# A decoder layer's middle: state space stage, sample attention and mixing as one program with interleaved engine orders

## The chip, the cores and the metric

The kernel runs on one core of one Trainium2 chip. The metric is the device time of one execution in microseconds (us), the median of the runs; less is better. A core has five engines that run on their own and meet only at semaphores: TensorE (PE, with its weight loads as PEld), VectorE (DVE), ScalarE (ACT), GpSimd (POOL) and SyncE (SP), which here issues most DMAs. All data are fp32.

## What is computed

One inference step of a hybrid decoder layer for a prompt of 1024 positions and a sample group of 8 sequences with 4 new positions each (32 rows). What matters here is the first sub-layer. One projection gives q, k, v and u; 12 heads of 64 in three groups attend with dilation 1, 4 and 16; u drives a diagonal state space model; both outputs are normalised, concatenated and go through w_out.

```python
def parallel_mixer(xn, pos, past_kv, s0_re, s0_im, p):
    z = xn @ p['w_in']                       # q | k | v | u
    ...
    for g, (win, dil) in enumerate(ATTN_GROUPS):      # (128,1), (512,4), (2048,16)
        if past_kv is None:
            o, lse = dilated_attn_prompt(qg, kg, vg, win, dil)
        else:                                # keys and values of the cache, then the new ones
            o, lse = dilated_attn_sample(qg, k_all, v_all, win, dil, buf.shape[1])
        outs.append(o); lses.append(lse)
    alpha = jax.nn.softmax(jnp.stack(lses, axis=2), axis=2)
    attn = jnp.stack(outs, axis=2) * alpha[..., None]
    y, h_re, h_im = s5_scan(u, s0_re, s0_im, p)       # h' = a h + b u ; y = Re(C h) + D u
    zs = jax.nn.gelu(y)
    ssm_out = zs * jax.nn.sigmoid(zs @ p['w_glu'] + p['b_glu'])
    mixed = concat([rmsnorm(attn), rmsnorm(ssm_out)])
    return mixed @ p['w_out'], ...
```

The outputs also include the last states of the model for the prompt and for each sample. After this come cross attention and a ConvFFN.

## The kernel before, in words

`build` calls one function per stage. Each opens a `Block`, in which every engine has its own instruction list, in the order in which the Python code emits it; no engine looks ahead in its own list, waits are semaphore thresholds (`wait_ge`), and all engines meet at the end of a block. The stages are `block_project` (L100: projection and prompt attention), `block_ssm` (L629), `block_sample` (L1153), `block_mix` (L1419), then `block_dense` for w_out, the memory projection and w_xq, cross attention, w_xo, and the FFN. This case is about the three in the middle. SBUF tensors of each are placed by nested scopes, and the eight PSUM banks are reused by all.

`block_ssm`. SP issues 10 loads for lambda, dt and B (L718 to L726), then C, the start states, D, the GLU weights and the gains (L730 to L737); TensorE and GpSimd wait for all 13 of the latter with one semaphore (`ld`). VectorE and ScalarE turn lambda and dt into a = exp(lambda dt) (L880 to L896; the sine wants another activation table). VectorE makes powers of a, B' and its chunk form BAR/BAI (L872 to L945, `bb`) and C times powers, CAR/CAI (to L957). GpSimd multiplies U by D (L766) and makes the table ER/EI of a^(8k) for the 128 chunks by doubling (L776 to L781, six instructions per complex product, two products per doubling). TensorE transposes C and the states (L1031, L1033), U (L1038), the sample's U (L1043) and BAR/BAI (L1050), makes the Toeplitz blocks (L1061), which SP spreads into TZ with 8 DMAs (L747), and the chunk sums (L1072, L1080). VectorE rotates the sums by the table (L966), scans them (L981, L982) and rotates back into HR/HI. TensorE then transposes the last states (L1088), computes the prompt's outputs (L1097 to L1100) and the sample's (L1108, L1110). GELU, the GLU product (L1121) with its sigmoid, and the norm (L1023) follow, each in a loop over 9 tiles of rows (8 of the prompt, 1 of the sample).

`block_sample`. 48 loads of cached keys (24) and then values (24) go through a ring of 12 slots, `ringS`; a slot is loaded again when TensorE has used what it held. The groups have 1, 4 and 2 blocks of 128 keys per sequence, 56 in all. For each, TensorE transposes two halves into one of four banks (L1363), ScalarE or VectorE in turn copies them to one of 8 places in `kTcS` (L1266, L1322), and TensorE multiplies three blocks later (L1372). The scores are transposed once, masked and put through a softmax over 128 partitions (L1330 to L1341), transposed back, and the values are weighed (L1409). Meanwhile GpSimd squares the attention outputs of the prompt (L1247), VectorE reduces them (L1315), and GpSimd sends the statistics through DRAM into row order (L1149).

`block_mix`. VectorE works out the mixing weights and norms (L1495 to L1519), then scales the 24 tiles of prompt attention (L1524), GpSimd multiplies by the gain (L1464), TensorE transposes each of 36 tiles (9 of the state space model, 3 of the sample, 24 of attention; L1542), ScalarE writes the high part XH (L1476) and VectorE the rest XL (L1492), through four banks. SP loads the first block of w_out.

Of the kernel before, what the change touches and what calls it, by code (L numbers as in the profile page):

```python
# [22 lines left out]
G = 3  # L23
# [13 lines left out]
def rows(t):  # L37

    return P if t < NT else TS
# [60 lines left out]
def block_project(nc, I, O, S):  # L100
# [19 lines left out]
    with ExitStack() as c:  # L120
# [103 lines left out]
        def _(sp):  # L224
# [6 lines left out]
            for i in range(TILES):  # L231
# [8 lines left out]
                if i in (1, 4):  # L240
                    load_weights(i // 4)
            stored, vs = [0] * 4, 0
# [386 lines left out]
def block_ssm(nc, I, O, S):  # L629

    ident, gain_bc, U, US, ysb = S["ident"], S["gain_bc"], S["U"], S["US"], S["ysb"]
    bank = S["bank"]
    (BpR, BpI, ER, EI, XR, XI, HR, HI, ta, tb, BAR, BAI) = S["ssm_over"]
# [5 lines left out]
    assert abs(PI_A + PI_B + PI_C - 2 * math.pi) < 1e-11  # L645

    with ExitStack() as c:
# [6 lines left out]
        lamR, lamI, dt_ = sb("lamR", [P, GH]), sb("lamI", [P, GH]), sb("dt_", [P, GH])  # L654
        Bin = sb("Bin", [P, 2, GH, 16])
        Cin = sb("Cin", [16, 2, 16, 64])
        Dbc = sb("Dbc", [P, SW])
        bglu = sb("bglu", [P, SW])
        wglu = sb("wglu", [P, 2, SW])
        USp = sb("USp", [DB, 16, CH, 16])  # L660
        sm = sb("sm", [P, 24, GH])
        PR, PI = sb("PR", [P, 9, GH]), sb("PI", [P, 9, GH])
        QR, QI = sb("QR", [P, 8, GH]), sb("QI", [P, 8, GH])
        CI_ = sb("CI_", [P, 2, GH, 16])
        H0 = sb("H0", [P, 2, GH, DB])
        CAR, CAI, WBR, WBI, TZ, UT, Sin = S["ssm_mats"]
        MZ = S["MZ"]
        UTs = sb("UTs", [P, 16, DB])
        FR = sb("FR", [P, 2, GH, 9])
        hout = sb("hout", [9, 2, D])  # L670
        YS8 = sb("YS8", [DB, DT, SW])
        nrm = sb("nrm", [P, 3, TILES])

        ld_lam = sem("ld_lam")
        ld = sem("ld")
        ld_us = sem("ld_us")
        us_zero = sem("us_zero")
        p_exp = sem("p_exp")
        p_ang = sem("p_ang")
# [1933 lines left out]
```

## Time and profile before

| | |
|---|---|
| median of 3 runs | 2240.26 us (2239.89 to 2257.68) |
| profiled execution | 2243.17 us, span 2241.5 us, granted TensorE clock 0.892 in the mean |
| PE busy | 1984.5 us, 89% |
| PEld / DVE / ACT / POOL busy | 82% / 44% / 30% / 12% |
| DMA | 125.24 MB, mean 56 GB/s |

The page divides the span into 40 slices of 56 us; digits are tenths of busy time, and for PEclk tenths of the full TensorE clock:

```
PE   5899999745698678879989989799999999999997
PEclk9999999855855589999999589899999999999998
```

The three stages lie in slices 9 to 15 (from 464 to 793 us). A clock digit of 5 is 1.2 GHz, full is 2.4 GHz; the "granted clock" of a stretch is its mean. In the timeline a row gives start, duration, engine, line, operation, output and inputs, count, and in brackets the idle time before it and what ended it. One fp32 product is recorded as two matmul records, a transpose as one.

### The profile page before, as it was taken

Reading aid. Unit: us, or ns where it says so; the run is one execution under the profiler, and the core shown is the slowest. Engines: PE = TensorE matmul, PEld = TensorE weight load, DVE = VectorE, ACT = ScalarE, POOL = GpSimd, SP = SyncE. Lnnn points to the kernel's source line nnn. Section 1 sums busy time; section 2 is a strip of 40 time slices with the busy share of each in tenths; the row PEclk is TensorE's granted clock in tenths of the full one; section 3 lists DMA queues with packets and bytes.
Section 4 is the critical chain, followed back from the end, with each engine's and each line's share of the span. In section 5 each row is a group of like instructions: output and inputs, shape, how many; then the busy total and the mean of one; then the engine's idle time right before and its main releaser. Section 6 shows DMA issues by size and latency. Waiting matters only on the chain. (4 is left out here: it accounts for less than half of the span.)

```text
span 2241.5 us, 32194 instructions
## 1 busy us (share of the span) xinstructions
PE 1984.5 (89%) x12704; PEld 1845.1 (82%) x12704; DVE 978.6 (44%) x2056; ACT 662.8 (30%) x1571; POOL 260.4 (12%) x596
## 2 busy tenths in 40 slices
PE   5899999745698678879989989799999999999997
PEld 5798989634498468879989988799889988899886
DVE  5515445444220543354345023455454455545453
ACT  5324243311311332244444012342132322232221
POOL 2504316034011200000000000000000000000000
PEclk9999999855855589999999589899999999999998
DMA  4101100011054043211032420121111202111102
GB/s 150 55 24 40 53 25 4 4 26 11 8 147 122 19 160 110 85 48 39 1 121 78 122 67 20 48 58 41 46 38 48 58 29 58 29 58 47 40 20 78
DMA packets 135728, 125.24 MB, mean 56 GB/s; under 512 B 15284, under 2 KB 128080, under 8 KB 135602
## 3 DMA queue, kind: packets, MB, share of 16 engines
q1 hardware_dynamic: 129986, 109.28, 16.3%
q0 software_dynamic: 5632, 14.44, 2.0%
q8 instruction: 75, 1.23, 0.2%
q14 instruction: 35, 0.29, 0.0%
HBM read 112.43 MB, written 10.60 MB: 55 GB/s over the span
## 5 line engine op out<-in xcount | busy, mean ns | idle before, releaser
L2382 PE MATMUL bank<-XH,WH 128*128 128x352 f32 x1056 | 343.6, 325 | 0.0
L2382 PE MATMUL bank<-XL,WH 128*128 128x352 f32 x1056 | 339.5, 322 | 0.0
L2382 PE MATMUL bank<-XH,WL 128*128 128x352 f32 x1056 | 339.2, 321 | 0.0
L1866 PE MATMUL bank<-WH,XH 128*128 128x256 f32 (+1 forms) x864 | 251.8, 291 | 18.7 <-DVE WL L1772 18.7
L1866 PE MATMUL bank<-WL,XH 128*128 128x256 f32 (+1 forms) x864 | 248.0, 287 | 0.0
L1866 PE MATMUL bank<-WH,XL 128*128 128x256 f32 (+1 forms) x864 | 246.3, 285 | 0.0
L616 PE MATMUL bank<-WH,XH 128*128 128x256 f32 (+3 forms) x648 | 211.5, 326 | 7.7 <-DVE WL L422 7.7
L2313 DVE TENSOR_TENSOR hres<-hres,bank 128x512 f32<-128x512 f32 (+1 forms) x198 | 135.6, 685 | 176.4 <-PE bank L2406 176.2
L616 PE MATMUL bank<-WL,XH 128*128 128x256 f32 (+3 forms) x648 | 203.6, 314 | 0.0
L616 PE MATMUL bank<-WH,XL 128*128 128x256 f32 (+3 forms) x648 | 202.4, 312 | 0.0
L2382 PEld LDWEIGHTS bank<-XH,WH 128*128 128x128 f32 x1056 | 199.1, 189 | 1.2
L2382 PEld LDWEIGHTS bank<-XL,WH 128*128 128x128 f32 x1056 | 199.3, 189 | 0.4
L2382 PEld LDWEIGHTS bank<-XH,WL 128*128 128x128 f32 x1056 | 198.8, 188 | 0.0
L1866 PEld LDWEIGHTS bank<-WH,XH 128*128 128x128 f32 (+1 forms) x864 | 159.6, 185 | 20.3 <-DVE WL L1772 19.6
L2406 PE MATMUL bank<-DH,AH 128*128 128x512 f32 (+1 forms) x396 | 158.9, 401 | 4.6 <-DVE co L2304 4.6
L1866 PEld LDWEIGHTS bank<-WH,XL 128*128 128x128 f32 (+1 forms) x864 | 160.2, 185 | 0.7
L1866 PEld LDWEIGHTS bank<-WL,XH 128*128 128x128 f32 (+1 forms) x864 | 159.6, 185 | 0.6
L2406 PE MATMUL bank<-DH,AL 128*128 128x512 f32 (+1 forms) x396 | 156.7, 396 | 0.0
L2406 PE MATMUL bank<-DL,AH 128*128 128x512 f32 (+1 forms) x396 | 156.5, 395 | 0.0
L616 PEld LDWEIGHTS bank<-WH,XH 128*128 128x128 f32 (+1 forms) x648 | 138.1, 213 | 11.3 <-issue 8.8
L616 PEld LDWEIGHTS bank<-WH,XL 128*128 128x128 f32 (+1 forms) x648 | 138.5, 214 | 1.9
L616 PEld LDWEIGHTS bank<-WL,XH 128*128 128x128 f32 (+1 forms) x648 | 138.6, 214 | 1.7
(440 smaller groups left out, 3435.1 us busy)
## 6 DMA issues: line engine op xcount, KB each, us to landing
wstage<-w_up SPq DMA_DIRECT2D x44, 512.0 KB, 5.2
ring<-cache_mem_kv SPq DMA_DIRECT2D x64, 256.0 KB, 2.9
dstage<-w_down POOLq DMA_DIRECT2D x22, 512.0 KB, 3.7
wstage<-w_in SPq DMA_DIRECT2D x10, 1024.0 KB, 5.1
ringS<-cache_kv_dil SPq DMA_DIRECT2D x16, 512.0 KB, 6.8
wstage<-w_xkv SPq DMA_DIRECT2D x8, 1024.0 KB, 5.4
ringS<-cache_kv_dil SPq DMA_DIRECT2D x48, 128.0 KB, 3.2
xin<-x_prompt SPq DMA_DIRECT2D x8, 512.0 KB, 3.5
```

The source lines that it names most:

```text
L616: ins = nc.tensor.matmul(out, x, w[:, :, k] if pair else w[:, load % 2, k], start=k == 0 and j == 0, stop=k == KT - 1 and j == 2)
L1866: ins = nc.tensor.matmul(MM[s % 3][:r, 0:WB], x[:, k, cols], w[:, b % 2, k], start=k == 0 and i == 0, stop=k == KT - 1 and i == 2)
L2313: nc.vector.tensor_tensor(dst, dst, bank[6 + u % 2][:rows(t)], ALU.add).then_inc(y, 1)
L2382: ins = nc.tensor.matmul(bank[3 * g + j][:, 0:CH], w[:, slot, k, P * g:P * g + P], x[:, k, CH * j:CH * j + CH], start=k == 0 and i == 0, s ...
L2406: ins = nc.tensor.matmul(bank[6 + u % 2][:r, :], x[:, s, P * t:P * t + r], w[:, s, 512 * half:512 * half + 512], start=s == 0 and i == 0, ...
```

## The change

The three functions become one, `block_middle`, with one `Block`. Every engine's list is written as an interleaving of the three stages' pieces.

TensorE's order is now: three of four U transposes; new-key scores; C and state transposes; the fourth U; keys of pairs 0 to 3; sample U; pairs 4 to 7; the B transposes; pairs 8, 9; chunk sums; pairs 10 to 15; Toeplitz products; pairs 16 to 21; sample outputs; prompt outputs 0, 1; pairs 22 to 27; score transposes; prompt outputs 2, 3; probability transposes; last states; values 0 to 19; nine gate steps with four value blocks each; then the 36 mixing tiles. Key blocks go in pairs through two banks (2 and 3), copied by ScalarE alone into a `kTc` of 2 x 4 halves; banks 4 to 7 serve the state space stage. The ring has 7 slots. The ten loads of lambda, dt and B are issued in `block_project`. GpSimd's table starts at a^8 and has one product per doubling. `QR`/`QI` are read as a reversed view of `PR`/`PI`. VectorE scans in place and works by halves of the groups; the squares of the attention outputs are ScalarE's. VectorE scales the attention tiles between its gate steps, and takes 12 attention tiles ahead of the state space tiles in the mixing.

```diff
--- block_project, SP, behind the loads of x
+            for half in range(2):
+                for dst, name in ((lamR, "ssm_lam_re"), (lamI, "ssm_lam_im")):
+                    sp.dma_start(dst[ps], ...).then_inc(S["ld_lam"], 16)
+                sp.dma_start(dt_[ps], ...).then_inc(S["ld_lam"], 16)
+                for j, name in enumerate(("ssm_b_re", "ssm_b_im")):
+                    sp.dma_start(Bin[ps, j], ...).then_inc(S["ld_lam"], 16)
--- SP
+            load_ring(0, 3)
             sp.wait_ge(us_zero, 1)
...
+            load_ring(3, RING)
...
+            load_ring(RING, 20)
             sp.wait_ge(tz, 4)
             sp.wait_ge(tz_zero, 1)
             for j in range(CH):
                 sp.dma_start(TZ[16 * j:16 * j + 16, :, 16 * j:P], MZ[:, :, 0:P - 16 * j]).then_inc(tz_st, 16)
+            load_ring(20, 24 + RING)
             sp.wait_ge(ys_c, 2)
...
+            load_ring(24 + RING, len(loads))
+            sp.dma_start(S["wstage"][:], weight_block(I, "w_out", 0)).then_inc(S["w_next"], 16)
--- GpSimd
-            m = 2
+            m = 1
             while m < NC:
-                half = ER[:, :, m // 2:m // 2 + 1], EI[:, :, m // 2:m // 2 + 1]
-                times(v[0], v[1], *half, *half, 1)
-                b = [x.to_broadcast([P, GH, m]) for x in v]
-                times(ER[:, :, m:2 * m], EI[:, :, m:2 * m], ER[:, :, 0:m], EI[:, :, 0:m], *b, m)
+                b = [y[:, :, m - 1:m].to_broadcast([P, GH, m]) for y in (ER, EI)]
+                ins = times(ER[:, :, m:2 * m], EI[:, :, m:2 * m], ER[:, :, 0:m], EI[:, :, 0:m], *b, m)
                 m *= 2
--- ScalarE
+            def take_keys(first, last):
+                for p in range(first, last):
+                    act.wait_ge(k_p, p + 1)
+                    if p >= 2:
+                        act.wait_ge(s_p, p - 1)
+                    nc.scalar.activation(kTc[:, p % 2], bank[2 + p % 2][:].rearrange(...), ACT.Copy).then_inc(k_a, 1)
+            def squares(g):
+                if g:
+                    act.wait_ge(s_rd, g)
+                nc.scalar.activation(sq[:], att[:, g * NT:g * NT + NT], ACT.Square).then_inc(s_sq, 1)
...
+            take_u(3)
+            squares(0)
+            take_keys(0, 4)
...
+            take_keys(8, 10)
+            squares(1)
+            take_keys(10, 13)
+            squares(2)
+            take_keys(13, 16)
--- VectorE
+            sum_squares(0)
...
+            dve.wait_ge(e_tab, 1)
+            for a in range(2):
+                dve.wait_ge(l_p, a + 1)
...
+                nc.vector.tensor_tensor(HI[:, gs, 1:NC + 1], HI[:, gs, 1:NC + 1], tB, ALU.add).then_inc(h_ok, 1)
...
+            sum_squares(1)
+            sum_squares(2)
...
+            scale(0, 6)
+            for j in range(TILES + 2):
+                if j < TILES:
+                    dve.wait_ge(gl_p, j + 1)
+                    nc.vector.tensor_tensor(gate(j)[:n], YB[2 + j % 2][:n, 0:SW], bglu[:n], ALU.add).then_inc(gl_s, 1)
+                if j >= 2:
+                    dve.wait_ge(sg, i + 1)
+                    nc.vector.tensor_tensor(ysb[:n, i], ysb[:n, i], gate(i)[:n], ALU.mult).then_inc(so, 1)
+                scale(6 + j, 7 + j)
+            scale(17, A)
--- TensorE
+            def keys(first, last):
+                for p in range(first, last):
+                    if p < KPAIRS:
+                        transpose_keys(p)
+                    if p == ls_pair + 1:
+                        pe.wait_ge(ls_r, 1)
+                    if p >= 1:
+                        scores(p - 1)
...
+            values(0, 20)
             pe.wait_ge(f_s, 4)
             pe.wait_ge(z_ok, 1)
+            pe.wait_ge(ld_g, 64)
...
                 if j:
                     gate_product(j - 1)
+                values(20 + 4 * j, 24 + 4 * j)
             gate_product(NT)
+            for k in range(3):
+                transpose_head(k)
             pe.wait_ge(o_c, 3)
...
+            for k in range(3, len(work)):
+                transpose_head(k)
--- build
-            S["ringS"] = o.enter_context(nc.sbuf_tensor("ringS", [P, 12, 4, GW], F32))
-            S["kTcS"] = o.enter_context(nc.sbuf_tensor("kTcS", [P, 8, 2, P], F32))
+                          so("EI", [P, 8, P]), so("kTcS", [P, 2, 4, P]), so("ringS", [P, 7, 4, GW]))
```

## Rows read from the trace of the kernel before

**Rows 1.** Stretches: length; busy PE, PEld, DVE, ACT, POOL; PEclk; DMA share; GB/s

```profile
557.00:574.00 17.00, 17.00 (x102) 13.01 (x100) 2.36 (x4) 0.59 (x2) 0.00 (x0) 1.00 0.00 1
...
617.10:683.80 66.70, 66.42 (x336) 65.72 (x337) 18.43 (x32) 11.38 (x32) 10.01 (x6) 0.50 0.53 153
683.80:693.80 10.00, 3.56 (x13) 2.01 (x13) 3.22 (x9) 3.12 (x13) 4.33 (x6) 0.50 0.26 52
693.80:745.20 51.40, 51.26 (x236) 50.78 (x236) 0.00 (x0) 1.61 (x9) 0.00 (x0) 0.50 0.30 82
745.20:768.00 22.80, 7.27 (x30) 4.59 (x30) 13.81 (x43) 12.03 (x26) 0.59 (x1) 0.50 0.14 46
768.00:792.80 24.80, 15.83 (x48) 6.92 (x48) 22.89 (x46) 13.30 (x24) 18.32 (x24) 0.50 0.00 0
```

**Rows 2.** Waits, middle part: engine line <- releaser: us, times, longest

```profile
PE bank L1031 <- DMA gain_bc<-ssm_out_norm: 22.4, 1, 22.4
...
PE bank L1088 <- DVE FR L992: 21.7, 1, 21.7
DVE XR L966 <- POOLq L796: 21.2, 1, 21.2
```

**Rows 3.** Timeline, TensorE, state space stage: start, duration, instructions

```profile
489.01 3.67 PE L1038 MATMUL bank<-ident,U 128*128 128x128 f32 x16
...
511.06 0.58 PE L1061 MATMUL bank<-CAR,BpR 64*16 64x128 f32 x2 [5.22 <-issue]
...
523.92 3.68 PE L1072 MATMUL bank<-UT,WBR 128*64 128x128 f32 x32
...
596.73 1.03 PE L1121 MATMUL bank<-wglu,zT 128*128 128x256 f32 x4
```

**Rows 4.** Timeline of SP and ScalarE: a weight load and its use, a copy

```profile
51.88 0.43 SPq L228 DMA_DIRECT2D wstage<-w_in  x1
...
83.23 2.18 ACT L311 ACTIVATE WH<-wstage 128x512 fp32r<-128x512 f32 x4
...
490.16 0.60 ACT L816 ACTIVATE UT<-bank 128x512 f32<-128x512 f32 x1 [0.43 <-PE bank L1038]
```

**Rows 5.** Timeline of GpSimd while it makes the table of powers

```profile
500.01 1.30 POOL L778 TENSOR_TENSOR XI<-ER,sm 128x16 f32<-128x16 f32 x1
...
511.16 0.24 POOL L778 TENSOR_TENSOR XI<-ER,sm 128x32 f32<-128x32 f32 x1
...
516.49 0.40 POOL L776 TENSOR_TENSOR XR<-ER,sm 128x128 f32<-128x128 f32 x1
...
530.71 1.27 POOL L781 TENSOR_TENSOR EI<-XI 128x512 f32<-128x512 f32 x1
```

**Rows 6.** Timeline of VectorE in the state space stage

```profile
506.60 1.40 DVE L872 TENSOR_TENSOR CAI<-PR,CI_ 128x1152 f32<-128x1152 f32 x1
...
533.33 0.68 DVE L968 TENSOR_TENSOR XI<-ER,bank 128x512 f32<-128x512 f32 x1
```

**Rows 7.** DMA of the cache ring: size, median us to landing; all loads

```profile
ringS<-cache_kv_dil SPq DMA_DIRECT2D x16, 512.0 KB, 6.8
...
DMA to landing us min/median/max: 2.0/4.4/12.2
```

**Rows 8.** Timeline of VectorE: normalisation, copies out of mixing, scales

```profile
610.26 3.64 DVE L1023 SCALAR_TENSOR_TENSOR ysb<-ysb,nrm,gain_bc 128x256 f32<-128x256 f32 x9
...
759.28 4.75 DVE L1492 TENSOR_TENSOR XL<-bank,XH 128x256 fp32r<-128x256 f32 x11
...
766.89 2.49 DVE L1524 TENSOR_TENSOR att<-att,w 128x256 f32<-128x256 f32 x4
```

**Rows 9.** Busy time in two stretches of the cross attention stage

```profile
1200.00:1220.00 20.00, 20.00 (x162) 19.38 (x161) 11.61 (x39) 9.28 (x24) 0.00 (x0) 1.00 0.28 81
1240.00:1260.00 20.00, 20.00 (x96) 20.00 (x95) 0.00 (x0) 0.00 (x0) 0.00 (x0) 0.50 0.51 154
```

**Rows 10.** Timeline of TensorE in the cross attention stage

```profile
1201.65 0.95 PE L2036 MATMUL bank<-qxT,kTx 128*128 128x4 f32 x8
```

More of the change, by code:

```diff
@@ L645, in block_ssm @@
     assert abs(PI_A + PI_B + PI_C - 2 * math.pi) < 1e-11
+    NTL = [1, 4, 2]
+    TOK = [4, 1, 2]
+    NKS = P + TS
+    RING = ring.shape[1]
+    loads = [(kv, g, b) for kv in range(2) for g in range(G) for b in range(DB)]
+    units = [(g, b, i) for g in range(G) for b in range(DB) for i in range(NTL[g])]
+    UNITS = len(units)
+    g_end = [8, 40, 56]
+    A = G * NT
+    SCORES = [(0, 0), (0, 2 * P), (1, 0)]
+    B4, B5, B6, B7 = bank[4:8]
+    UB = (B5, B6, B7, B5)
+    QB = (B5, B6, B7, B4)
+    YB = (B7, B4, B5, B6)
     with ExitStack() as c:
@@ new lines, in _ @@
+            take_keys(22, KPAIRS)
+            act.wait_ge(w_sub, 1)
+            nc.scalar.activation(w1[:], w1[:], ACT.Exp).then_inc(w_ex, 1)
+            for g in range(G):
+                b_, c0 = SCORES[g]
+                act.wait_ge(s_p, KPAIRS)
+                act.wait_ge(s_n, G)
+                nc.scalar.activation(sT[:, g, 0], bank[b_][:, c0:c0 + P], ACT.Copy)
+                nc.scalar.activation(sT[0:TS, g, 1], bank[b_][0:TS, c0 + P:c0 + 2 * P], ACT.Copy).then_inc(s_c, 1)
+            act.wait_ge(mx, 1)
@@ new lines, in _ @@
+            dve.wait_ge(n_q, 1)
+            nc.vector.tensor_scalar(nrs[:, 1:2], nrs[:, 0:1], 1.0 / AW, EPS, ALU.mult, ALU.add).then_inc(n_m, 1)
+            for k in range(6, 10):
+                take_rest(k)
+            dve.wait_ge(n_r, 1)
+            link(nc.vector.reciprocal(nrs[:, 3:4], nrs[:, 2:3]))
+            nc.vector.scalar_tensor_tensor(attS[:], attS[:], nrs[:, 3:4], gain_bc[0:TS, 0:AW],
+                                           ALU.mult, ALU.mult).then_inc(as_n, 1)
+            for k in range(10, len(work)):
+                take_rest(k)
@@ new lines, in scores @@
+            def scores(p):
+                pe.wait_ge(k_a, p + 1)
+                for u in (2 * p, 2 * p + 1):
+                    g, b, i = units[u]
+                    b_, c0 = SCORES[g]
+                    for hp in range(2):
+                        out = bank[b_][:, c0 + 64 * hp:c0 + 64 * hp + 64].rearrange("p (h n) -> p h n", h=2)
+                        ins = nc.tensor.matmul(out[:, :, tokens(g, b, i)], kTc[:, p % 2, 2 * (u % 2) + hp],
+                                               Qbd[:, g, hp, :, tokens(g, b, i)], start=True, stop=True)
+                ins.then_inc(s_p, 1)
@@ new lines, in _ @@
+            for q in range(3):
+                transpose_u(q)
+            pe.wait_ge(q_bd, 2)
+            for g in range(G):
+                b_, c0 = SCORES[g]
+                for hp in range(2):
+                    ins = nc.tensor.matmul(bank[b_][0:TS, c0 + P + 64 * hp:c0 + P + 64 * hp + 64], qkS[:, g, 1, hp],
+                                           Qbd[:, g, hp].rearrange("p h n -> p (h n)"), start=True, stop=True)
+                ins.then_inc(s_n, 1)
+            pe.wait_ge(ld_c, 64)
@@ L1084, in _ @@
[L1084 to L1085 removed]
+            ins.then_inc(ls_p, 1)
+            keys(10, 16)
+            pe.wait_ge(ca, 1)
             for q in range(4):
[L1087 to L1093 removed]
+                pe.wait_ge(l_r, q // 2 + 1)
+                ps = slice(64 * (q // 2), 64 * (q // 2) + 64)
```

1149 lines of the change are left out of this document (534 added, 615 removed).

## The prediction, made before the result was known

> **What bounds the kernel now.** I read the page first: TensorE is busy for 89% of the span, but the slices between about 460 and 800 us show it at 4 to 9 tenths and at a granted clock of 0.5 to 0.8, while the dense stages around them show 9 and 1.0. All that the diff rewrites lies there, so the next view was the busy time by stretch [rows 1]. It shows a key stage (617.1 to 683.8) in which TensorE is busy 66.4 of 66.7 us, a gap of 10 us, a value stage (693.8 to 745.2, 51.3 of 51.4 us), and the mixing (745.2 to 792.8), where TensorE works 23 of 47.6 us; ahead of them, from 485 on, is the state space stage, in which the page's slices show no engine full. The middle starts at 463.9 and its last VectorE instruction ends at 792.8: 328.8 us. Then the waits: in the first part TensorE stands 22.4 us behind the last load of the stage and 21.7 us behind a VectorE chain, and that chain stood 21.2 us behind GpSimd's table of powers [rows 2]. Each stage is a chain of one engine at a time; keys and values are the only parts in which TensorE itself is the limit. So the question is what TensorE's own queue needs when the three stages share it, and which waits remain in that queue.
>
> **The change, by TensorE's new order.** Little TensorE work is removed; it is reordered. I walk its queue from the start of the block (0 = 463.9) and add only what ends each step.
>
> Head, 10.9. The ten parameter loads now stand in the projection, so the angle chain starts at once. One activation table load (1.3) and short steps bring the zeroed query block at 4.9; three of the four U transposes run before that. Then the new-key scores 1.5, the 32 small C and state transposes 3.5 and the last four U transposes 0.9 (a quarter of 3.67 [rows 3]). The C loads have 6.4 us to land, at worst 3 more. SP's ten moved issues filled 463.9 to 474.9, 10.9 us; in the projection they come before the third weight load, issued at 51.9 and first read at 83.2 [rows 4]: 31.3 us of room. I cost them at nothing; without that room they would cost up to 10.9.
>
> Keys, 66.7 + 1.4. 56 key blocks (28 pairs) at the measured stretch. The copy of a pair is now always ScalarE's, 128x512 in 0.6 us [rows 4], and has the scores of the pair before (8 records of 0.21, 1.7 us) as cover, so two banks in the place of four cost nothing in the steady state. The first pair waits: ScalarE has three U copies, the C copies and a 1.9 us squaring ahead of it, 1.4.
>
> State space matrices on TensorE: 1.9 for the sample U, 3.5 for the 16 transposes of B, 8.2 for the chunk sums (32 products in 6.2 and the sample ones in 2.1), 13.0 for the Toeplitz products at the low clock [rows 3].
>
> A new wait, 10.6. ScalarE copies keys up to pair 12, then squares group 2; that squaring waits until VectorE has reduced group 1 (one buffer), and VectorE does that only behind both halves of the scan. Behind it in ScalarE's queue are key copies 13 to 15, and TensorE waits for those. When: GpSimd's table starts at 5.5. It had 90 operations, now 60. While VectorE streams two-input operations, a GpSimd operation on 128x16 takes 1.30 us; on 128x32, with VectorE still, 0.24 [rows 5]. VectorE's big operations end at 27.9 (six of 1.26, six of 1.4 from 11.8, bb at 19.4); by then all but the three largest doublings are done. Those ran from 516.5 to 532.0 [rows 5], 15.5 us with two steps of six small operations (1.2 each) between that the change drops: 13.1, and 1 for VectorE's reduction beside them, so the table ends at about 42. TensorE's first chunk sums are there at 43. So neither waits for the other by much. Then VectorE needs twice 10.1 (four 128x512 with a bank operand at 0.6, two adds 1.25, eight scans 2.5, four products 2.4, two adds 1.25 [rows 6]) and 0.4: 63.7. Reduction 2.3, squaring 1.9, copy 0.6: 68.7. TensorE got there at 58.1 (48.0 and five transposed, four scored pairs). Bounds: 0, if the table and the products were 10 us earlier; 20, if GpSimd loses its slot for longer, by the 21.2 us that VectorE waited for it before [rows 2]. I take 10.6, the working of its rows.
>
> The Trainium skill, GPSIMD Engine Reference, section Specifications, says that GpSimd's SBUF interfaces are shared with VectorE and that VectorE instructions with two SBUF inputs contend. The trace agrees (1.30 against 0.24), and this speaks against the change, because the VectorE chain is moved onto the table's early steps. Priced as though every one of the 60 operations met it, the table would end at 5.5 + 60 x 1.3 = 83.5, 40 us later; the rows deny that, since VectorE has no such work from 30 to 43.
>
> Then the sample outputs 10.2 at the low clock (8.6 at the full one) and the prompt outputs 18.6 (17.0 for all four at the full clock [rows 3], plus 0.8 in each of two starts at the low one). The Toeplitz DMAs (7.6 to issue, some 3.5 to land) lie beside keys 16 to 21 (14 us). Sample scores' transposes 1.9; the softmax (about 8.4 up to the scaled probabilities, with the mixing weights threaded between) lies beside prompt outputs 2 and 3 (9.3): this is where the 10 us gap [rows 1] goes. Transposed probabilities 1.3, final states 3.3.
>
> Values, 51.3, and gates, 19.4. 20 of 56 value blocks run first, four after each gate step. A gate step is two transposes and four records of a product, 2.15 at the low clock, twice the 1.08 between its products at the full one (1.03 busy [rows 3]), nine of them. GELU, sigmoid, the products and GpSimd's gains lie beside it. The ring has 7 slots in the place of 12: at the start of the values loads 24 to 30 (of 0 to 47) are there, and load j waits for the release of j-7. The 512 KB loads landed in 6.8 us median [rows 7], issued six ahead; one is consumed per four blocks, 3.7 us. I cost this at nothing; the bounds are 0 and 15, two or three late landings.
>
> Tail, 12.7 + 19.7. After the last gate VectorE has 10 scales (0.62 each) and 3 products left, 8.1, then mean, root and reciprocal 1.0, and nine normalisations 3.6 [rows 8]. This is late now where a 23 us stretch was before. 36 mixing tiles follow with VectorE free of the scales: 0.43 to 0.55 us each [rows 8], 18.2, and 1.5 for the sample norm in between. Nothing of the final barrier or of the next stage's first 7 us changes.
>
> Sum: 10.9 + 66.7 + 1.4 + 1.9 + 3.5 + 8.2 + 13.0 + 10.6 + 10.2 + 18.6 + 1.9 + 1.3 + 3.3 + 51.3 + 19.4 + 12.7 + 19.7 = 254.6. Against 328.8 that saves 74.2. The profiled execution took 2243.2 (span 2241.5 and 1.7 around it), so 2169; the median shown is 2240.3, 2.9 lower, and the forecast on that footing is 2166. About 1% is what a measurement of this kernel can tell from no change; this is 3.3%.
>
> **Rivals.**
> 1. The clock. The value stage runs at granted 0.50 (1.2 GHz). In the cross stage, where such small products stand between dense ones, the granted clock is 1.00 and eight of their records take some 0.83 [rows 9, 10]; the same stage without the dense ones falls to 0.50 [rows 9]. The change puts 36 value blocks between gate products. At the full clock a block costs 0.41 in the place of 0.92, a gate step 1.08 in the place of 2.15: 36 x 0.51 + 9 x 1.07 = 28 less, 2138. For it: the cross rows. Against: a gate step is 2.15 of 5.8 us, and the key stage, with a third to 40% of its time in transposes, stays low. The Trainium skill, TensorE: Matmul & The Clock Gate, section What's actually happening, goes further: the clock is released by how busy TensorE has been. If that held here, the key and value stages would have been at 2.4 GHz before; they were full for 66 and 51 us and at 0.50 [rows 1], so the rows disagree. Were it so in the new block, with keys at 0.62 and values at 0.41 a block, 32 us and 28 would go beside the 10, about 2096.
> 2. More new waits than I found: one in-order queue per engine now serves three stages, with 17 hand-placed switches on TensorE. The wait for ScalarE at 20, the value ring at 15, the C loads at 3 in the place of nothing: about 20 to 27 more, 2190. For it: SP is in order too, and the ring's loads stand behind Toeplitz and sample stores. Against: each of these has some 5 us of room by the steps above.
> 3. Slower than before: the ring. If the 17 loads behind the seventh slot were each fully exposed because a slot is given back just before its data are wanted, each would cost its landing, 6.8 at 512 KB [rows 7]: 17 x 6.8 = 116, less the 74, gives 2282. It decides from 4.4 us a load on. For it: the old ring held 12, and the longest landing was 12.2. Against: six loads are always under way ahead of the one in use, and the stage moved 82 GB/s against 153 in the key stage [rows 1].
> 4. It does not do what it says, that is, the stages run one after another all the same, because TensorE's order ties them: then only the 22 us of loads and about 15 of barriers and heads go, 2203. Against: no wait in the queue reaches over a whole stage.
>
> **How the numbers follow.** Forecast 0.55 (2150 to 2182), clock at the gates 0.20 and clock everywhere 0.04, more waits 0.16, one after another 0.04, slower 0.01. The likeliest is 2166. The range goes down to 2130, below the gate clock case, and up to 2193, over the more-waits case; clock everywhere, one after another and slower lie outside. Faster by over 1% means below 2218: 0.98; within 1%: 0.01; slower: 0.01.
>
> **What would show it.** In the profile after: the middle's last VectorE write some 255 us after its start; TensorE waiting for ScalarE's key copy once for about 10 us, with VectorE's second half of the scan running; no TensorE wait over 3 us for a ring load; the same 66 and 51 us of key and value work in pieces; granted clock 0.5 in keys and gates, 1.0 in the prompt outputs; and a tail of some 32 us behind the last gate product with VectorE nearly full. Wrong it would be with a clock of 1.0 in the gates (then 28 less), with TensorE idle on the cache loads in the values, or with the table ending 20 us later than the chunk sums. Sizes most in doubt are the ScalarE wait and the tail; everything after the middle should be as before.

## The result, and the profile after

| | before | after |
|---|---|---|
| median, same chip | 2241.47 us (4 runs, 2239.89 to 2257.68) | 2182.47 us (4 runs, 2180.10 to 2188.32) |
| profiled execution, span | 2243.17, 2241.5 | 2188.32, 2186.6 |
| middle, block start to last VectorE instruction | 328.8 | 271.6 |
| next stage's first product, from the block start | 336.1 | 278.9 |

The ratio is 0.971, 95% interval 0.967 to 0.976: 2.9% faster. Forecast were 2166, 74.2 less than before; the medians show 59.0 less, the two profiled executions 54.9, of which the middle gave 57.2. The other 2.3 lie ahead of the middle, which began at 463.9 in the profile of before and at 466.3 in that of after. Nothing shows them to be the change's: in the profiles of the twelve kernels below the middle began anywhere from 463.6 to 469.4, and at 466.4 in the one that has the loads back in the middle.

The page of the kernel after, busy tenths of TensorE and its granted clock in 40 slices (of 54.7 us each; the middle lies in slices 9 to 14):

```profile
PE   5899999877999689789899897899999999999997
PEclk9999999955555699999998699899999999999999
```

TensorE is at 7 tenths or more in all slices of the middle but the last, which holds the mixing. The clock is now at 5 for five slices on end; before, an 8 stood among the low ones, and that was the slice of the prompt outputs.

Busy time by stretch of the kernel after (columns as in [rows 1]): chunk sums, Toeplitz products, sample outputs, prompt outputs 0 and 1, keys 22 to 27, prompt outputs 2 and 3, gates with values, the stretch behind the last gate product, the rest of the mixing:

```profile
508.40:515.80 7.40, 7.40 (x130) 7.36 (x131) 3.51 (x6) 1.04 (x1) 5.62 (x3) 0.75 0.12 38
542.00:554.90 12.90, 12.90 (x66) 8.61 (x65) 1.11 (x5) 1.76 (x3) 4.56 (x6) 0.50 0.20 30
569.70:583.00 13.30, 13.30 (x97) 6.57 (x96) 0.00 (x0) 0.59 (x1) 0.00 (x0) 0.50 0.04 13
583.00:598.00 15.00, 15.00 (x50) 11.41 (x49) 0.69 (x1) 0.59 (x1) 0.00 (x0) 0.50 0.00 0
598.00:614.60 16.60, 16.58 (x81) 16.50 (x80) 0.69 (x1) 5.31 (x8) 0.00 (x0) 0.50 0.18 50
617.00:632.00 15.00, 15.00 (x49) 11.40 (x48) 7.08 (x22) 5.70 (x12) 0.00 (x0) 0.50 0.00 0
660.00:704.00 44.00, 43.89 (x174) 39.30 (x174) 7.56 (x22) 6.47 (x16) 5.80 (x8) 0.50 0.18 56
704.00:718.00 14.00, 3.21 (x14) 2.32 (x14) 13.56 (x28) 8.72 (x37) 8.41 (x10) 0.50 0.00 1
718.00:738.00 20.00, 15.24 (x66) 9.15 (x64) 17.33 (x40) 16.31 (x38) 0.00 (x0) 0.67 0.00 0
```

Read the first two columns (length, busy TensorE): TensorE is full in every one of these stretches up to 704. The seventh column (the granted clock) says at which rate. The prompt outputs ran at 1.00 in [rows 1] (557 to 574); here the same instructions are at 0.50, and a group of six matmul records takes 1.88 us (583.00 to 584.88) where it took 1.06.

The waits of the middle, as waiting engine and line <- releaser: us in all, times, longest:

```profile
PE bank L1338 <- ACT kTcS L915: 17.5, 2, 16.2
ACT sq L926 <- DVE st L1149: 15.7, 1, 15.7
...
DVE XR L1168 <- PE bank L1399: 12.2, 1, 12.2
...
PE bank L1548 <- ACT oS L1036: 10.4, 1, 10.4
...
PE bank L1365 <- DVE Qbd L1081: 3.6, 1, 3.6
```

No other single wait of TensorE inside the middle is over 1.2 us. The first two are one wait, the forecast's "new wait". ScalarE's timeline shows it: the last line holds two key copies, the first of which TensorE stands for, and the line above it the squaring that stands in front of them.

```profile
518.95 0.60 ACT L915 ACTIVATE kTcS<-bank 128x512 f32<-128x512 f32 x1 [0.68 <-PE bank L1327]
535.27 1.91 ACT L926 ACTIVATE sq<-att 128x2048 f32<-128x2048 f32 x1 [15.72 <-DVE st L1149]
537.08 1.07 ACT L915 ACTIVATE kTcS<-bank 128x512 f32<-128x512 f32 x2
```

VectorE reduces group 1 only behind both halves of the scan, and that is when the squaring may start. VectorE's timeline, its first read of the chunk sums, the second half's last operation and the reduction:

```profile
512.26 0.69 DVE L1168 TENSOR_TENSOR XR<-ER,bank 128x512 f32<-128x512 f32 x1 [12.19 <-PE bank L1399]
...
532.35 0.68 DVE L1185 TENSOR_TENSOR HI<-HI,R 128x512 f32<-128x512 f32 x1
532.95 2.28 DVE L1149 TENSOR_REDUCE st<-sq 128x32 f32<-128x2048 f32 x1
```

### The profile page after: what moved, and what is told of

It reads as the page before. It is cut to its first block and busy times, and to the rows that moved or that the text cites. A ratio compares the mean times of both kernels' runs of the same rounds, so it can differ in the third digit from the quotient of the medians.

```text
span 2186.6 us, 32100 instructions
## 1 busy us (share of the span) xinstructions
PE 2000.3 (91%) x12704; PEld 1858.5 (85%) x12704; DVE 965.2 (44%) x2020; ACT 671.7 (31%) x1575; POOL 245.6 (11%) x561
## 5 line engine op out<-in xcount | busy, mean ns | idle before, releaser
L1873 PEld LDWEIGHTS bank<-WH,XH 128*128 128x128 f32 (+1 forms) x864 | 159.8, 185 | 20.2 <-DVE WL L1779 19.5
```

The lines of the kernel that those rows point to most:

```text
L1873: ins = nc.tensor.matmul(MM[s % 3][:r, 0:WB], x[:, k, cols], w[:, b % 2, k], start=k == 0 and i == 0, stop=k == KT - 1 and i == 2)
```

## The experiments

All were run beside the kernel before. "Middle" is the time from the block start to the first product of the next stage in the kernel's profile (278.9 after); it leaves out how long the projection happened to take. The wait for the first weights of the next stage was 8.6 to 8.8 us in every profile. The runs were made on three chips: experiments 1 to 4 on one, on which the kernel before took 2246.5 us (median of 7); outputs together, loads back, ring of 4 and all three on a second (2243.1, of 7); the last four rows of the table on a third (2256.5, of 11, from 2240.1 to 2265.8). Between these groups the middle compares best; the microseconds and the ratios only as far as the scatter of the kernel before allows, and the kernel after was timed only in the run of the result.

| run | median (range) | ratio to before, 95% | middle |
|---|---|---|---|
| after | 2182.5 (2180.1 to 2188.3) | 0.971, 0.967 to 0.976 | 278.9 |
| squares later | 2169.2 (2165.5 to 2170.7) | 0.965, 0.961 to 0.969 | 262.1 |
| outputs copied first | 2181.5 (2178.6 to 2185.8) | 0.971, 0.967 to 0.975 | 277.0 |
| states first | 2172.0 (2169.1 to 2180.3) | 0.966, 0.962 to 0.970 | 268.5 |
| gates together | 2169.0 (2165.0 to 2171.8) | 0.964, 0.960 to 0.968 | 260.5 |
| outputs together | 2182.1 (2170.8 to 2184.4) | 0.972, 0.968 to 0.976 | 282.1 |
| loads back | 2197.8 (2195.7 to 2201.1) | 0.980, 0.977 to 0.982 | 291.6 |
| ring of 4 | 2187.0 (2182.9 to 2190.5) | 0.975, 0.972 to 0.977 | 283.2 |
| all three | 2133.5 (2129.6 to 2134.9) | 0.951, 0.948 to 0.954 | 226.2 |
| squares and outputs | 2149.4 (2146.9 to 2151.8) | 0.955, 0.950 to 0.960 | 245.8 |
| squares, states, gates | 2141.9 (2132.8 to 2153.9) | 0.950, 0.945 to 0.956 | 246.3 |
| transposes twice | 2164.1 (2161.0 to 2167.6) | 0.961, 0.956 to 0.966 | 265.1 |
| gates at once | 2135.2 (2131.2 to 2138.5) | 0.948, 0.944 to 0.952 | 230.1 |

**1. Squares later.** Is the 16 us wait the squaring's alone?

```diff
             take_keys(10, 13)
-            squares(2)
             take_keys(13, 16)
             for q in range(4):
                 act.wait_ge(tz_p, q + 1)
...
+            squares(2)
             take_keys(16, 22)
```

> ScalarE squares group 2 only behind the four copies of the Toeplitz blocks, not ahead of the copies of key pairs 13 to 15. My theory: the 16.2 us for which TensorE stands behind a key copy is the wait of that squaring for VectorE's reduction, and nothing else of the chain is needed that early: VectorE has read the second half of the chunk sums at 525.2, and TensorE gets to the Toeplitz products at about 526. So the 16.2 us go and no wait over 1 us takes its place: 2182.5 - 16 = 2166 to 2168. The rival (another wait takes over, because the keys run only from VectorE's slack): TensorE then stands 5 us or more for VectorE or for the Toeplitz store, and the time is 2172 to 2183.

Measured: 2169.2, 1 us over the theory's range, the middle 16.8 shorter, and TensorE's list of waits holds nothing in its place (the 1.3 is the first key pair's, which the kernel after has too):

```profile
PE bank L1548 <- ACT oS L1036: 10.4, 1, 10.4
PE bank L1365 <- DVE Qbd L1081: 3.6, 1, 3.6
PE bank L1338 <- ACT kTcS L915: 1.3, 1, 1.3
```

The theory holds; the rival would show another wait of 5 us or more here.

**2. Outputs copied first.** The other long wait in TensorE's list, 10.4 us for ScalarE's copies of the sample outputs. The edit moves the loop that writes `oS` (with its `act.wait_ge(v_p, UNITS)`) from behind the square root of `nrm` to right behind the gate loop.

> ScalarE copies the sample attention outputs (12 small copies, 2.4 us) right behind the last gate, ahead of the nine squarings, the table load and the root. TensorE stands 10.4 us for these copies in the kernel after. My theory: the wait is only a sign, VectorE is what the tail waits for (13.6 of the 14.0 us from 704 on are busy, and it takes the first rest of a mixing tile only behind its nine normalisations), so this gives 0 to 1.5 us: 2181 to 2183, TensorE's wait falls to 1 to 3 us and as much comes back as a wait for VectorE's XL. The rival, that the wait is the price: the 10.4 us go, less some 2, that is 2173 to 2175.

Measured: 2181.5. The wait changed its name and kept its size:

```profile
PE bank L1540 <- DVE XL L1297: 9.4, 1, 9.4
...
PE bank L1548 <- ACT oS L1021: 1.2, 1, 1.2
```

The waits of that kernel from 700 us on: 10.4 became 1.2 and 9.4. Compare the stretch 704 to 718 of the kernel after: VectorE 13.56 of 14.00. TensorE's wait named ScalarE; the bound was VectorE. The middle is 1.9 shorter; the medians, 1.0 apart, don't resolve it.

**3. States first.** The granted clock. Before, the 16 transposes of the last states stood ahead of the prompt outputs; here they are in TensorE's timeline, and then the stretch in which they end (columns as in [rows 1]):

```profile
553.72 3.25 PE L1088 MATMUL bank<-ident,FR 128*9 128x128 f32 x16 [21.71 <-DVE FR L992]
```

```profile
554.00:557.00 3.00, 3.00 (x18) 2.11 (x16) 0.00 (x0) 1.70 (x3) 0.00 (x0) 0.58 0.00 0
```

TensorE had stood idle for 21.7 us at 0.50. The first output began at 556.81, and between 556.00 and 556.80 the granted clock was already 0.69 in the mean: it rose in the last transposes.

```diff
             keys(16, 22)
             pe.wait_ge(tz, 4)
             pe.wait_ge(tz_st, 16 * CH)
+            pe.wait_ge(f_ok, 1)
+            for q in range(4):
+                for g in range(4):
+                    ins = nc.tensor.transpose(YB[q][0:9, P * g:P * g + P], FR[:, q // 2, 4 * (q % 2) + g], ident[:])
+                ins.then_inc(f_p, 1)
...
             prompt_y(0)
             prompt_y(1)
+            pe.wait_ge(f_s, 4)
+            for l in range(2):
...
+                ins.then_inc(ysm_p, 1)
             keys(22, KPAIRS + 1)
```

The same loop of transposes goes from behind those of the probabilities, and that of the sample outputs (`for l`) from ahead of `prompt_y(0)`. `prompt_y` waits for the copy of its bank (`f_s`), ScalarE's copies move along, and `hout` lies in the space of `WBR`/`WBI`.

> The 16 transposes of the last states go ahead of the prompt outputs 0 and 1, and the sample outputs behind these: the order of TensorE's work that the kernel before had, where the granted clock went from 0.50 to 1.00 in the transposes and stayed there for outputs at 1.05 us a group of six. Theory A (what runs just ahead decides the level): the clock rises here too, prompt outputs 0 and 1 take 8.5 in the place of 15.0 us and the sample outputs 8.6 in the place of 13.4: 11 us less, 2171 to 2173; if 2 and 3 rose also, 6 more. Theory B (the stretch of keys before, all at 0.50, holds the clock down whatever follows): it stays at 0.50 and the time is 2180 to 2184.

Measured: 2172.0. By stretch: the transposes; prompt outputs 0 and 1 with the sample outputs; the first keys behind; prompt outputs 2 and 3:

```profile
572.00:576.00 4.00, 4.00 (x20) 2.65 (x20) 0.00 (x0) 2.12 (x4) 0.00 (x0) 0.50 0.12 39
576.00:592.40 16.40, 16.40 (x143) 11.06 (x142) 1.38 (x2) 0.81 (x2) 0.00 (x0) 1.00 0.00 1
592.40:600.00 7.60, 7.60 (x59) 7.56 (x56) 0.00 (x0) 3.28 (x6) 0.00 (x0) 0.77 0.26 71
609.00:624.00 15.00, 15.00 (x52) 11.33 (x51) 7.12 (x24) 5.70 (x12) 0.00 (x0) 0.50 0.00 0
```

Read the granted clock down: 0.50 in the transposes, 1.00 behind them, down again among the keys. The 28.3 us of outputs became some 17. That is theory A, in this execution, and the median lies in its range.

**4. Gates together.**

```diff
                 if j:
                     gate_product(j - 1)
-                values(20 + 4 * j, 24 + 4 * j)
             gate_product(NT)
+            values(20, UNITS)
```

VectorE's `scale(6 + j, 7 + j)` and `scale(17, A)` become `scale(6, A)` behind the gate loop.

> The nine gate steps follow one another behind value block 20, and the other 36 value blocks stand behind them; VectorE scales its 18 attention tiles behind the gates. Theory: the interleaving of the gates gave TensorE nothing, since it is full either way, but it put the norm of the state space output behind the last value block. With the gates first, scales, squares, root and normalisations (14 us behind the last gate in the kernel after) lie beside 33 us of values: the mixing starts right behind the values and takes some 20, so the 33.5 us of tail become 20 to 22: 12 to 13 less, 2169 to 2171. If the gates, now dense, are granted the full clock, as they were in the kernel before, another 8 to 10 go: 2160. The rival (the waits between the engines inside a gate step now show, as nothing stands between the steps): each of nine steps costs 1 to 2 us more and eats the gain: 2175 to 2185.

Measured: 2169.0, the middle 18.4 shorter. By stretch, the first gates, the others, the values and the mixing:

```profile
655.00:659.00 4.00, 3.95 (x11) 3.07 (x11) 0.42 (x1) 1.78 (x4) 0.00 (x0) 0.50 0.22 66
659.00:668.00 9.00, 9.00 (x49) 6.80 (x48) 5.75 (x16) 5.56 (x17) 0.00 (x0) 0.97 0.01 3
668.00:697.00 29.00, 29.00 (x144) 28.87 (x144) 15.42 (x33) 5.43 (x23) 19.52 (x18) 0.53 0.31 94
697.00:720.00 23.00, 18.66 (x78) 12.11 (x76) 16.32 (x37) 19.33 (x53) 0.00 (x0) 0.55 0.00 0
```

Both mechanisms of the theory show: the third line has VectorE's 15.4 and GpSimd's 19.5 us of scales and norms beside full TensorE, and the second line has the gates at full clock, though only from the third step on. The time from the last value block to the end of the mixing's transposes is 23.0 (it was 34), and the nine gate steps take 13.1 where they took 19.4. But with the clock's part the theory had 2160, and the medians lie 13.5 apart (the profiled executions 16.6, the middles 18.4): each part gave less than forecast. The rival's waits inside the gate steps don't show.

**5. Outputs together.** The keys first, then score transposes, last states, prompt outputs 0 and 1, sample outputs in banks 0 and 1, prompt outputs 2 and 3.

```diff
-            keys(16, 22)
+            keys(16, KPAIRS + 1)
             pe.wait_ge(tz, 4)
             pe.wait_ge(tz_st, 16 * CH)
+            for g in range(G):
+                pe.wait_ge(s_c, g + 1)
...
-            keys(22, KPAIRS + 1)
...
             prompt_y(2)
             prompt_y(3)
```

The transposes of the states stand behind those of the scores; VectorE takes the prompt outputs behind the softmax.

> All keys first (pairs 16 to 28), then the score transposes, the last states, prompt outputs 0 and 1, the sample outputs (in banks 0 and 1) and prompt outputs 2 and 3 without keys between; VectorE's softmax lies beside them. Theory: the stretch of keys between the outputs is what takes the granted clock back to 0.50 (in the run with the states first it fell some 4 us into keys 22 to 27, and prompt outputs 2 and 3 then took 15.0 us behind six short transposes). With the four outputs behind the last states the clock stays at 1.00 for all of them: 17.0 us in the place of 30.1, sample outputs 8.6 in the place of 13.4, 18 less than the kernel after, 7 less than the run with the states first: 2164 to 2166. Rival A: the clock falls again anyway inside a stretch of 26 us: 2168 to 2173. Rival B: the softmax, now later, holds TensorE before the values for 3 us or more.

Measured: not the theory. 2182.55, 2184.42 and 2181.63 in three executions and 2170.76 in one, with mean granted clocks of 0.900, 0.898 and 0.900 in the three and 0.906 in the one, whose time is in the range of rival A; in the profile (the 2182.55) all outputs are at 0.50, right behind the same 16 transposes that had 1.00 behind them in experiment 3:

```profile
589.20:632.20 43.00, 43.00 (x194) 29.09 (x192) 5.33 (x17) 7.35 (x15) 0.00 (x0) 0.50 0.01 1
```

43 us in which TensorE is full, at half the clock. So the transposes are no guarantee.

**6. Squares and outputs; squares, states and gates; transposes twice.** Three runs on what decides it. The first two combine edits shown; the third adds to "states first":

```diff
             keys(22, KPAIRS + 1)
...
+            pe.wait_ge(ys_c, 2)
+            for r in range(16):
+                nc.tensor.transpose(YB[2 + r // 8][0:9, P * (r % 4):P * (r % 4) + P], FR[:, r // 8, r % 8], ident[:])
             prompt_y(2)
             prompt_y(3)
```

> The later squaring and the outputs together, without the gates. Up to the gates this is the program of all three, whose outputs were granted the full clock in all four executions (2130 to 2135), while the outputs together without the later squaring were at 0.50 in the profile and in three of four executions (2182 to 2184, one at 2171). Theory A: the 17.9 us idle stretch of TensorE, 55 us ahead of the outputs, is what made the difference (with it gone the level rises in the last states every time): all executions at 2147 to 2151. Theory B: whether the clock rises there is chance, from one execution to the next: a spread of more than 10 us between the executions, 2149 for some and 2165 for others.

> The later squaring, the states first (keys 22 to 27 still between the outputs) and the gates together. By the spans of the middle: 16.8, 10.4 and 18.4 less, 45.6: 2137. If prompt outputs 2 and 3 were at the full clock also, 2131; if the states did not raise it, 2147. Against all three with the outputs together (2133): 3 to 5 us slower by my account, since two of the prompt outputs cost 15.0 in the place of 8.5.

> The kernel with the states first, and the 16 transposes of the last states once more ahead of prompt outputs 2 and 3, their results overwritten: 3.6 us of work that computes nothing. Theory A (such transposes, 128 rows by 128 columns each, raise the granted clock wherever they stand): prompt outputs 2 and 3 take 8.5 in the place of 15.0 us, 6.5 less for 3.6 more: 2168 to 2170. Theory B (they do nothing by themselves): the level stays at 0.50 and the time is 3.6 above the kernel with the states first: 2175 to 2176.

Measured: 2146.9 to 2151.8 for the first, all four within 1 us of theory A's range. For the second 2153.9, 2147.5, 2136.3 and 2132.8, with mean granted clocks of 0.907, 0.907, 0.912 and 0.915: a spread of 21 us in one kernel, and its profile (the 2153.9) has the outputs at 0.50 behind the transposes. Experiment 3 puts the two levels of those outputs at 11 us, so they can't be all of the 21, and the other three executions have no trace. The third run's middle is 3.4 shorter than that of "states first", where theory A had 2.9, and its prompt outputs 2 and 3 took 9.2 in the place of 15.0 (its 2164.1 and the 2172.0 of "states first" are from different chips). The stretches with all or part of the outputs: first run, second run; and of the third its added transposes and prompt outputs 2 and 3:

```profile
573.00:598.20 25.20, 25.20 (x194) 17.75 (x193) 5.24 (x17) 7.35 (x15) 0.00 (x0) 1.00 0.01 2
```

```profile
554.40:582.40 28.00, 28.00 (x146) 17.68 (x144) 2.49 (x7) 1.17 (x2) 0.00 (x0) 0.50 0.01 3
```

```profile
602.40:606.00 3.60, 3.60 (x18) 2.44 (x18) 3.26 (x8) 2.08 (x7) 0.00 (x0) 0.50 0.00 0
606.00:615.00 9.00, 9.00 (x49) 6.86 (x49) 3.91 (x14) 3.62 (x6) 0.00 (x0) 0.91 0.00 0
```

What follows: ahead of outputs at 1.00 those 16 transposes stood each time; without them (the kernel after and experiments 1, 2, 4, 7 and 8) the prompt outputs never got there. But with them it is not certain either: the level rose to 1.00 behind them in six stretches of five profiles (experiment 3, the first and third run here, "all three", "gates at once") and stayed at 0.50 in two (experiment 5 and the second run here). The six kernels that keep the transposes behind prompt outputs 2 and 3 bear this out: in all six profiles the level, 0.50 through 15 us of full outputs, rose in these transposes or up to 1 us behind them, and fell again among the value blocks 3 to 7 us later. With the kernel before that is 13 rises in 15 stretches. Nor does it take these transposes: in the kernel after the level rose inside the chunk sums (0.50 from 510 to 512, 0.96 from 512 to 514), behind key blocks at 0.50. The mean granted clocks of experiment 5's and the second run's executions say that one kernel can differ from one execution to the next, but not in which stretch. What settles it in an execution stays open. Theory A's reason, the idle stretch of TensorE ahead, is not it either: the second run here has no such stretch and stayed low, experiment 3 has one and rose.

**7. Loads back.** Was it right to cost the ten moved loads at nothing where they went? The diff of `block_project` is undone, and the same ten lines stand at the head of SP's list in the middle.

> The ten loads of lambda, dt and B are issued at the head of the middle again, as in the kernel before, all else as after. Theory (moving them took 10.9 us off the head and cost nothing in the projection): the angle chain starts some 10 us later, so the new-key scores and the keys behind them start 8 to 11 us later. But the table of powers, the first half of the scan and ScalarE's late squaring move by as much, so nothing gives it back: 2191 to 2194. Rival: the loads cost the projection 2 to 3 us where they stand now (the middle began 2.4 us later in the profile of the kernel after than in that of before), so the projection gets these back here and the loss is only 5 to 8 us: 2187 to 2190, with the middle starting at 464.

Measured: 2197.8, 15.3 above the kernel after by the medians, more than either theory; the middle is 12.7 longer and began at 466.4, not at 464. Waits at its head:

```profile
PE bank L1365 <- DVE Qbd L1081: 17.4, 1, 17.4
...
DVE sm L1066 <- ACT dt_ L930: 17.3, 1, 17.3
ACT dt_ L930 <- DMA Bin<-ssm_b_im: 15.4, 1, 15.4
```

The ten issues took 9.7 us (10.9 in the kernel before), and ScalarE stood until the last of them had landed, 15.4 us. TensorE's wait grew from 3.6 to 17.4, by 13.8, of which 1.1 came back further on. A cost where they stand now doesn't show: TensorE's waits for the projection's weights are 7.7 us in the profiles of before, after and this run alike, and the loss is far over the rival's 5 to 8. The rival falls.

**8. Ring of 4.** The slower rival said the ring.

```diff
-... so("ringS", [P, 7, 4, GW]))
+... so("ringS", [P, 4, 4, GW]))
```

> Four slots in the ring of cached keys and values in the place of seven, all else as after. Theory: a load has the work of three loads as cover, 14.7 us of keys or 11 us of values at 512 KB against 7.3 us to land, so the loads themselves cost little (0 to 4 us, in the groups with one and two blocks a load). What costs is SP's order: the store of the Toeplitz blocks stands behind load 19, which now waits for key pair 20 in the place of 14, so that TensorE stands some 7 to 9 us for it ahead of the sample outputs. 2190 to 2196. Rival (the ring itself was close to its edge, my case on the other side): every load behind the fourth slot is exposed for half its landing or more: 20 value loads at 3.5 us, over 2240.

Measured: 2187.0, 4.5 more and below the theory's range. Its executions overlap with those of the kernel after, so the medians alone don't tell the two apart; the middle is 4.3 longer. TensorE's waits that are new in it:

```profile
PE bank L1430 <- DMA TZ<-R: 4.2, 1, 4.2
...
PE bank L1487 <- DMA ringS<-cache_kv_dil: 2.2, 2, 1.4
...
PE bank L1327 <- DMA ringS<-cache_kv_dil: 0.8, 1, 0.8
```

The largest is the Toeplitz store behind a load in SP's order, as the theory had it, at half its size; the waits for the cache loads themselves are 3.0 in sum. Of these 7.2 us 4.3 reached the length of the middle. Seven slots have slack, and the rival (over 2240) falls.

**9. All three.** Squares later, outputs together, gates together; and, last, "gates at once": the same with 4 value blocks ahead of the gates in the place of 20, and the square root for the mixing weights behind the copies of the probabilities.

> The later squaring, the outputs together and the gates together in one kernel. If the three gains are separate they add up: 16.8 (squaring), 18 (outputs) and 18.4 (gates and tail), by the spans of the middle, 53 less: 2129 to 2133. If one gain was the cover of another (the softmax beside outputs that are now short; the gates' full clock, which came behind value blocks), 5 to 15 of it are lost: 2135 to 2148.

> All three changes, with the gates behind 4 value blocks in the place of 20, and ScalarE's root for the mixing weights moved behind its copies of the transposed probabilities. Theory: the wait ahead of the values (2.3 us) falls by about 1; the gates start some 6 us behind the prompt outputs, while the clock is still at 1.00, so that their first three steps take 1.1 in the place of 2.15 us (3 less); against this TensorE waits some 2 to 3 us for the GELU behind the fourth value block. 2129 to 2132. Rival: the clock falls in the four value blocks and the gates pay the rise again: 2133 to 2136.

Measured: 2133.5, at the upper end of the range for gains that add up; the middle is 52.7 shorter (16.8, 16.3 and 19.6 as the runs add them one by one). All four executions lie within 5.3 us, and the outputs in the profile are at 1.00:

```profile
575.20:600.30 25.10, 25.10 (x193) 17.66 (x193) 5.26 (x17) 7.35 (x15) 0.00 (x0) 1.00 0.01 2
```

"Gates at once" is 2135.2 (6 executions), the same within what is measured: the rival. Its gate steps stood at 0.77 in the mean and took 13.4 us, against 12.8 in "all three". "All three" is thus faster than both kernels: 4.9% below before, and 49 us below after by the medians, 46 by the ratios.

## Why the prediction was right, and where it was off

The forecast of the middle was 254.6 and 271.6 was measured, 17.0 more; less saved, but the signs and the mechanism held. The 2182.5 lies inside the stated range, yet at the edge of the band that was called likeliest (2150 to 2182), and nearer to the 2190 of rival 2 than to 2166. Term by term, in us (each rounded, so the column measured adds up to 0.2 more):

| term | forecast | measured |
|---|---|---|
| head | 10.9 | 12.4 |
| keys, with the first wait | 68.1 | 65.9 |
| sample U, B transposes, chunk sums | 13.6 | 12.9 |
| wait behind ScalarE | 10.6 | 16.2 |
| Toeplitz products | 13.0 | 12.9 |
| sample outputs | 10.2 | 13.3 |
| prompt outputs | 18.6 | 30.0 |
| small transposes, last states | 6.5 | 6.4 |
| values and gates | 70.7 | 67.9 |
| tail | 32.4 | 33.9 |

- **Prompt outputs**, +11.4, and **sample outputs**, +3.1: this is the term that failed. The step was "17.0 for all four at the full clock [rows 3], plus 0.8 in each of two starts at the low one" (the row is in [rows 1]). It took a duration from a stretch at 1.00 and took for granted that the products would bring the clock up by themselves within a start of a microsecond or two. The kernel before had 16 transposes of the last states in front, the change put those behind, and without them in front the outputs stayed at 0.50 in all six profiles. Experiment 3 got 11 back on prompt outputs 0 and 1 and the sample outputs by this order alone, in its profiled execution.
- **The wait**, +5.6. Its mechanism was right in each link, and experiment 1 shows it to be one. GpSimd's table ended 43.1 after the start, forecast 42; VectorE's first read came at 46.0 (forecast 43), since TensorE's first half of the chunk sums ended then. The wait so ended 2.7 later than forecast. And TensorE arrived 2.9 sooner, because the clock went up in the chunk sums (0.75 in that stretch) and the four key pairs behind them ran at it, 1.3 us each in the place of 2.45. The sooner it arrives, the longer it stands.
- **Head**, +1.5: the zeroed query block was there at 6.3, not 4.9.
- **Keys, values and gates**: mostly at 0.50, so the value of 0.92 a block and 2.15 a gate step carried. That both terms came out 2 to 3 us under the forecast is luck: the key pairs behind the chunk sums saved some 5 us, and the first 2 us of the values ran at 1.00, neither of which the sum had. Rival 1 (clock up in the gates) did not come in this order; it came from the third step on when the gates stood together (experiment 4).
- **What was costed at nothing**: the ten loads (experiment 7 shows 12.7 us gained in the middle and no cost seen in the projection), the ring of 7 (experiment 8), the key copies through two banks (beside the long wait only the forecast one of the first pair, 1.3 against 1.4), the Toeplitz store (no wait with seven slots).
- **The tail** was right in size (33.9 against 32.4), and VectorE was its engine, as forecast. But its working took the order as given: that 14 us of norms stood behind the last value block only because the gates were spread over the values was there to be seen, and experiment 4 gets 11 of it back.
- **Rival 2** (more new waits): no further one came that cost the middle, but its 20 us for the wait behind ScalarE were nearer to the measured 16.2 than the 10.6 of the sum. **Rival 3**: falls by experiment 8. **Rival 4** (one after another): no, TensorE is all but full from 542 to 704.

## What to carry to other kernels

Where stages are merged into one in-order queue, ask of each wait not which engine it names but what stands ahead of the awaited instruction in that engine's list: one squaring ahead of three key copies cost 16 us, and seven instructions later it cost nothing. Put work that feeds a long chain of other engines ahead of the bulk that can cover it (gates ahead of values), rather than sprinkled through it. A wait's length is no price either: the 10.4 us for ScalarE became 9.4 for VectorE when its named cause was moved (experiment 2). And a duration read from a trace holds only with its clock: take the level together with what stood in front, and if the change reorders that, carry both levels as bounds.

## What the runs showed of the hardware that was not expected

- Full TensorE is not enough for the full clock. 43.0 us of products without a gap stood at 0.50 in experiment 5, and 28.0 in "squares, states, gates", while the instructions of experiment 5, in the same order of TensorE's work, stood at 1.00 for 25.2 us in "squares and outputs"; the two kernels differ only in where one squaring stands in ScalarE's list. The Trainium skill, TensorE: Matmul & The Clock Gate, section What's actually happening, ties the clock to how busy TensorE has been; these rows don't agree with that alone.
- Transposes alone can raise it: in the kernel before, behind 21.7 idle us at 0.50, the level rose before TensorE had run anything but the 16 transposes.
- One kernel can take more than one course: executions of "squares, states, gates" lie at 2132.8 and 2153.9 (mean granted clock 0.915 and 0.907), of "outputs together" at 2170.8 and 2184.4 (0.906 and 0.898). The kernel before does it as well: eleven executions on one chip lie between 2240.1 (0.895) and 2265.8 (0.882). A single profile then says little of the clock in such a stretch.
- Beside VectorE's large two-input operations (128x1024 and 128x1152, 1.2 to 1.4 us each) GpSimd's small operations take 1.2 to 1.4 us as well, be they 128x16, 128x32 or 128x64: about as long as the VectorE operation that they stand beside. So the number of operations, not the elements, sets the table's early part. Once VectorE is at a reduction with one input, the same 128x64 takes 0.32. The kernel after, GpSimd's timeline and then VectorE's:

```profile
479.34 0.27 POOL L866 TENSOR_TENSOR XI<-EI,ER 128x16 f32<-128x16 f32 x1
479.69 1.18 POOL L867 TENSOR_TENSOR ER<-XR 128x16 f32<-128x16 f32 x1
...
491.30 1.43 POOL L864 TENSOR_TENSOR XR<-EI 128x64 f32<-128x64 f32 x1
...
495.61 0.32 POOL L867 TENSOR_TENSOR ER<-XR 128x64 f32<-128x64 f32 x1
```

```profile
479.56 1.22 DVE L1058 TENSOR_TENSOR WBR<-PR,BpR 128x1024 f32<-128x1024 f32 x1
...
491.22 1.36 DVE L1058 TENSOR_TENSOR CAI<-PR,CI_ 128x1152 f32<-128x1152 f32 x1
...
495.28 2.28 DVE L1149 TENSOR_REDUCE st<-sq 128x32 f32<-128x2048 f32 x1
```
